# Hyena filter spectra from folded taps, with the frequencies ordered by parity

## The reference

```python
def _hyena_filter(L, p):                 # L = 256, HY_WIDTH = 512
    ...
    filt = (hdn @ p['hy_w3']).reshape(L, 2, HY_WIDTH)
    decay = jnp.exp(-t * jnp.abs(deltas))
    return filt * decay[:, None, :]

def _long_conv(u, filt, bias):
    taps = jnp.concatenate([filt[:, 0], jnp.zeros((1, HY_WIDTH)), filt[:0:-1, 1]], axis=0)
    kf = jnp.fft.rfft(taps, n=2 * L, axis=0)
    uf = jnp.fft.rfft(u, n=2 * L, axis=1)
    y = jnp.fft.irfft(uf * kf[None], n=2 * L, axis=1)[:, :L]
    return y + u * bias
```

## Time and profile before

| what | us |
|---|---|
| median of 3 runs | 1240.18 |
| lowest and highest run | 1238.13, 1241.17 |
| span of the profiled execution, first to last instruction | 1237.0 |
| PE busy in it | 1199.5 |
| DVE busy | 821.1 |
| ACT busy | 523.2 |

### The profile page before, as it was taken

How to read it: one execution, slowest core, us unless ns; L and a number is a source line. 1 busy time by engine, 2 the same in 40 slices (tenths; PEclk the granted TensorE clock), 3 DMA queues, 4 the chain that set the end, 5 groups by cost and what they waited for, 6 DMA issues and landing times. The chain is left out here.

```text
span 1237.0 us, 16729 instructions
## 1 busy us (share of the span) xinstructions
PE 1199.5 (97%) x6774; PEld 961.6 (78%) x6774; DVE 821.1 (66%) x1287; ACT 523.2 (42%) x907; POOL 1.7 (0%) x8
## 2 busy tenths in 40 slices
PE   6999999999999999999999999999999998999998
PEld 4666877777677788888887788778888788889887
DVE  5654357969766737767656656566589876776674
ACT  4452535452544432322122223347566455443454
POOL 0000000000000000000000000000000000000000
PEclk9999999999999999999999999999999999999999
DMA  9832333421011155555565454323343223665653
GB/s 337 274 120 85 131 125 113 161 85 51 18 35 52 53 172 182 188 204 181 181 213 187 154 185 164 94 68 102 103 119 120 69 62 111 201 186 183 186 179 120
DMA packets 132388, 171.82 MB, mean 139 GB/s; under 512 B 9268, under 2 KB 112342, under 8 KB 132312
## 3 DMA queue, kind: packets, MB, share of 16 engines
q1 hardware_dynamic: 131828, 170.58, 42.6%
q10 hardware_dynamic: 484, 0.18, 0.1%
HBM read 169.69 MB, written 1.05 MB: 138 GB/s over the span
## 5 line engine op out<-in xcount | busy, mean ns | idle before, releaser
L1812 DVE TENSOR_TENSOR w_lo<-w_raw,w_hi 128x1024 fp32r<-128x1024 f32 (+1 forms) x220 | 263.7, 1203 | 173.6 <-ACT w_hi L1439 171.5
L1439 ACT ACTIVATE w_hi<-w_raw 128x1024 fp32r<-128x1024 f32 (+1 forms) x220 | 228.4, 1042 | 337.5 <-DMA w_raw<-in_w_gu_dram 141.9
L700 PE MATMUL ps<-h_hi,w_hi 128*128 128x512 f32 (+1 forms) x576 | 218.7, 380 | 1.5 <-DVE xbc L1984 1.0
L702 PE MATMUL ps<-h_hi,w_lo 128*128 128x512 f32 (+1 forms) x576 | 212.6, 369 | 0.0
L701 PE MATMUL ps<-h_lo,w_hi 128*128 128x512 f32 (+1 forms) x576 | 212.4, 369 | 0.0
L700 PE MATMUL ps<-f_hi,w_hi 128*128 128x512 f32 (+1 forms) x472 | 167.7, 355 | 2.1 <-DVE xT L2216 1.6
L702 PE MATMUL ps<-f_hi,w_lo 128*128 128x512 f32 (+1 forms) x472 | 162.5, 344 | 0.0
L700 PEld LDWEIGHTS ps<-h_hi,w_hi 128*128 128x128 f32 x576 | 108.5, 188 | 27.7 <-issue 9.4
L702 PEld LDWEIGHTS ps<-h_hi,w_lo 128*128 128x128 f32 x576 | 108.4, 188 | 18.7
L701 PEld LDWEIGHTS ps<-h_lo,w_hi 128*128 128x128 f32 x576 | 108.6, 189 | 17.4
L711 PE MATMUL ps<-h_hi,w_hi 128*128 128x512 f32 x320 | 113.2, 399 | 0.4 <-ACT gate L1744 0.4
(11 more groups left out here) (342 smaller groups left out, 1905.0 us busy)
## 6 DMA issues: line engine op xcount, KB each, us to landing
w_raw<-in_w_gu_dram SPq DMA_DIRECT2D x88, 512.0 KB, 3.5
w_raw<-in_w_in_dram SPq DMA_DIRECT2D x60, 512.0 KB, 3.7
w_raw<-in_w_down_dram SPq DMA_DIRECT2D x32, 512.0 KB, 3.5
m_even<-in_w_mod_dram SPq DMA_DIRECT2D x14, 1024.0 KB, 5.7
m_odd<-in_w_mod_dram SPq DMA_DIRECT2D x14, 1024.0 KB, 5.7
m_raw<-in_w_mod_dram SPq DMA_DIRECT2D x24, 512.0 KB, 5.5
m_first<-in_w_mod_dram SPq DMA_DIRECT2D x16, 512.0 KB, 10.1
w_raw<-in_w_out_dram SPq DMA_DIRECT2D x16, 512.0 KB, 3.4
```

The costliest lines, as they stand in the source:

```text
L700: mm(o, w_hi[:, i % RING, w], hi[:, 0:n], start=first and k == 0, stop=False)
L702: last = mm(o, w_lo[:, i % RING, w], hi[:, 0:n], start=False, stop=final and k == nk - 1)
L1439: A(w_hi[:, i % RING, w], w_raw[:, i % RING, w], ACT.Copy).then_inc(w_hi_done, 1)
L1812: TT(w_lo[:, i % RING, w], w_raw[:, i % RING, w], w_hi[:, i % RING, w].bitcast(F32), ALU.subtract).then_inc(w_lo_done, 1)
```

## The change

The taps are folded once more before they meet the table. A tap of lag t and its mirror image at lag 256 - t have the same cosine at even frequencies and the opposite one at odd frequencies (and the other way round for sines). So the second block of lags is laid out as the mirror image of the first, and the sum and the difference of the blocks are formed on DVE: four new rows `plus`, `minus`, `odd_sum`, `even_diff` in `t_folds`, and a changed `t_diff`. Lag 0 and lag 128, which have no partner, are handled by columns of signs. The frequencies are ordered by parity (multiples of 4, then the other even ones, then the odd ones), in the inverse tables too. Then each spectrum needs 128 folded lags in place of 256: three spectra are one product each, and two (c = 0 and c = 4) are two products with 64 output rows each, from `plus` and `minus`.

`c_fwd` shrinks from 2 x 768 to 643 columns; three of these are the sign columns. `taps_ready` is signalled behind the fold in both layers. The core of the diff:

```diff
-    fwd = np.concatenate([cos, alt, sin[:, 1:], 0 * alt, sin[:, 1:P], alt, cos[:, 1:P]], axis=1)
-    fwd = fwd.reshape(2, P, 6 * P).transpose(1, 0, 2)
+    even, odd = np.concatenate([np.arange(0, L, 4), np.arange(2, L, 4)]), np.arange(1, L, 2)
+    order = np.concatenate([even, odd])
+    angle = 2 * np.pi * np.arange(P)[:, None] * order / (2 * L)
...
+    fwd = np.concatenate([cos, sin, nyquist, 1.0 - 2.0 * first, first - 1.0, 1.0 - first], axis=1)
...
+    lags = np.concatenate([np.arange(P + 1), np.arange(L - 1, P, -1)])
...
-        c_fwd = at("c_fwd", 187, [2, 6 * P])
+        c_fwd = at("c_fwd", 187, [5 * P + 3])
...
+        t_folds = [at(f"t_fold{l}", kb, [4, 512]) for l, kb in enumerate((104, 156))]
...
+                def spectrum_of_taps(c, bank):
+                    plus, minus, odd_sum, even_diff = (t_folds[l][:, j, :] for j in range(4))
+                    if c in (0, 4):
+                        for half, src in enumerate((plus, minus)):
+                            last = mm(ps[64 * half:64 * half + 64, bank, :], c_fwd[:, c * P + 64 * half:c * P + 64 * half + 64], src,
+                                      start=True, stop=True)
+                    else:
+                        src = (odd_sum, even_diff, (t_diff, t_diff1)[l][:, 0, :])[c - 1]
+                        last = mm(ps[:, bank, :], c_fwd[:, c * P:(c + 1) * P], src, start=True, stop=True)
+                    p.sig(last, "spectra_psum")
...
-                    col, src = ((0, t_sum), (P, t_sum), (4 * P, t_diff), (3 * P, t_diff), (5 * P, t_sum))[c]
-                    for t in range(2):
-                        last = mm(ps[:, ACC, :], c_fwd[:, t, col:col + P], src[:, t, :], start=(t == 0), stop=(t == 1))
-                    p.sig(last, "spectra_psum")
+                    spectrum_of_taps(c, ACC)
...
-                    for b, col, src in ((0, 0, t_sum1), (1, P, t_sum1), (2, 4 * P, t_diff1), (3, 3 * P, t_diff1), (7, 5 * P, t_sum1)):
-                        for t in range(2):
-                            last = mm(ps[:, b, :], c_fwd[:, t, col:col + P], src[:, t, :], start=(t == 0), stop=(t == 1))
-                        p.sig(last, "spectra_psum")
+                    for c, bank in enumerate((0, 1, 2, 3, 7)):
+                        spectrum_of_taps(c, bank)
...
+            def fold_taps(l, sums, diffs):
+                plus, minus, odd_sum, even_diff = (t_folds[l][:, j, :] for j in range(4))
+                sign, other, rest = (c_fwd[:, 5 * P + j:5 * P + j + 1] for j in range(3))
+                p.link(TT(even_diff, diffs[:, 0, :], diffs[:, 1, :], ALU.subtract))
+                p.link(TT(plus, sums[:, 0, :], sums[:, 1, :], ALU.add))
+                p.link(STT(out=minus, in0=sums[:, 1, :], scalar=sign, in1=sums[:, 0, :], op0=ALU.mult, op1=ALU.add))
+                p.link(STT(out=odd_sum, in0=sums[:, 1, :], scalar=other, in1=sums[:, 0, :], op0=ALU.mult, op1=ALU.add))
+                p.settle()
+                p.sig(STT(out=diffs[:, 0, :], in0=diffs[:, 0, :], scalar=rest, in1=diffs[:, 1, :], op0=ALU.mult, op1=ALU.add), "taps_ready")
...
-                        p.sig(TT(t_sum[0:1, 0, :], t_sum[0:1, 0, :], t_hyb[0:1, :], ALU.add), "taps_ready")
+                        p.chain(TT(t_sum[0:1, 0, :], t_sum[0:1, 0, :], t_hyb[0:1, :], ALU.add))
+                        dve.wait_ge(consts_full, 64)
+                        fold_taps(0, t_sum, t_diff)
                         p.own("taps_ready")
...
-                        p.sig(TT(t_sum1[0:1, 0, :], t_sum1[0:1, 0, :], t_hyb1[0:1, :], ALU.add), "taps_ready")
+                        p.chain(TT(t_sum1[0:1, 0, :], t_sum1[0:1, 0, :], t_hyb1[0:1, :], ALU.add))
+                    else:
+                        fold_taps(1, t_sum1, t_diff1)
```

More of the change, by code:

```diff
@@ L210, in constants @@
     k = np.arange(L)[None, :].astype(np.float64)
-    cos, sin = np.cos(2 * np.pi * k * t / (2 * L)), np.sin(2 * np.pi * k * t / (2 * L))
     alt = (-1.0) ** t
-    fwd = np.concatenate([cos, alt, sin[:, 1:], 0 * alt, sin[:, 1:P], alt, cos[:, 1:P]], axis=1)
-    fwd = fwd.reshape(2, P, 6 * P).transpose(1, 0, 2)
+    even, odd = np.concatenate([np.arange(0, L, 4), np.arange(2, L, 4)]), np.arange(1, L, 2)
+    order = np.concatenate([even, odd])
+    angle = 2 * np.pi * np.arange(P)[:, None] * order / (2 * L)
+    cos, sin = np.cos(angle), np.sin(angle)
+    sin[0, P:] = np.sin(np.pi * odd / 2)
+    nyquist = np.concatenate([alt[:P], cos[:, 1:P]], axis=1)
+    first = (i == 0)[:, None]
+    fwd = np.concatenate([cos, sin, nyquist, 1.0 - 2.0 * first, first - 1.0, 1.0 - first], axis=1)
     w = np.where(k == 0, 1.0, 2.0)
     mid = 2 * np.pi * k * (t[:P] - (L - 1) / 2) / (2 * L)
-    fold = np.concatenate([np.cos(mid), alt[:P], np.sin(mid)[:, 1:]], axis=1).reshape(P, NFREQ, P)
-    unfold = np.concatenate([(np.cos(mid) * w).T, alt[:P].T, 2 * np.sin(mid)[:, 1:].T], axis=0) / (2 * L)
+    fold = [np.cos(mid), np.concatenate([alt[:P], np.sin(mid)[:, 1:]], axis=1)]
+    unfold = [(np.cos(mid) * w).T / (2 * L), np.concatenate([alt[:P].T, 2 * np.sin(mid)[:, 1:].T], axis=0) / (2 * L)]
+    fold = np.concatenate([v[:, order] for v in fold], axis=1).reshape(P, NFREQ, P)
+    unfold = np.concatenate([v[order] for v in unfold], axis=0)
     inv = np.concatenate([fold, unfold.reshape(NFREQ, P, P).transpose(1, 0, 2)], axis=1)
+    lags = np.concatenate([np.arange(P + 1), np.arange(L - 1, P, -1)])
     tl = np.linspace(0.0, 1.0, L, dtype=f4)[:, None]
@@ L223, in constants @@
     arg = (fl * wl).astype(f4).astype(np.float64)
-    feats = np.concatenate([tl, np.cos(arg), -np.sin(arg)], axis=-1).T
+    feats = np.concatenate([tl, np.cos(arg), -np.sin(arg)], axis=-1)[lags].T
     deltas = np.linspace(np.log(1e-2) / 1.5, np.log(1e-2) / 0.3, 512, dtype=f4)
-    decay = np.exp((-tl * np.abs(deltas)).astype(f4).astype(np.float64)).reshape(2, P, 512).transpose(1, 0, 2)
+    decay = np.exp((-tl * np.abs(deltas)).astype(f4).astype(np.float64))[lags].reshape(2, P, 512).transpose(1, 0, 2)
     freq = (10000.0 ** (-np.arange(0, 32, 2) / 32)).astype(f4)
@@ L2400, in half_taps @@
                 def half_taps(t):
-                    if t == 1:
-                        p.own("taps_ready")
-                    else:
+                    if t == 0:
                         dve.wait_ge(wdt_split, 2)
```

## The result

Medians: 1240.11 us before (22 runs, 1238.13 to 1243.84) and 1243.50 us after (22 runs, 1239.99 to 1247.84). The ratio is 1.0023, with an interval of 1.0016 to 1.003: some 2 to 4 us slower, which is less than the 0.3% that the prediction took as the least difference a measurement can tell, and above its 1241.5 us. Beside the last experiments the changed kernel came out at 1.0032 (1.0018 to 1.0046). So five products a layer are gone, 8 us of work by the prediction's count, and the kernel is not faster at all.

The account below looks back on a forecast made before the run. TensorE, busy 97% of the span, was taken as the bound. Terms -0.4 - 0.7 + 0 + 2 x 1.2 = +1.3 on a 1237.0 us span gave 1238.3, plus 3.2 to the median: 1241.5 us, range 1237.0 to 1245.0.

Parts of the forecast that it names:

- The clock: Behind PE's gaps in layer 0 and at layer 1's start: clock falls, +1.2 us each, ends 0 and 2.3.
- The smaller table: Near the program's start: c_fwd shrinks from 768 to 322 KB, so weights queued behind it come sooner, -0.4 us.
- Layer 0 without the clock: Layer 0's spectra: fold on PE's path +3.3 us, fewer products -4.0 us, together -0.7 us.
- The products of layer 1: Layer 1's start: products end earlier, but PE waits for the same copy until 808.5; gain 0, new gap 4.2 us.
- The fold in the feed-forward part: Layer 1's fold behind L2414: of 3.3 us, 1.0 fits in front and 2.3 push DVE, covered; cost 0.
- rival by which layer 1 pays: Layer 1's start: copies come as soon as their products, L804 starts 4 us earlier without gap; 1235 us, chance 0.04.
- case without falls: Both PE gaps, layer 0 and layer 1's start: neither lets the clock fall; 1239.1 us, chance 0.10.
- slower rival: Both gaps: low clock wholly on work, 2.3 us each, table gives nothing, fold takes 3.7; 1244.5 us, chance 0.10.

Follow-up runs that it names:

- fold added: Kernel before with the five fold instructions added, unread, ahead of `taps_ready` in layer 0, products and table unchanged: 1245.50 us, ratio 1.0047.
- table padded: Changed kernel with the table c_fwd padded with zeros to its old 768 KB: 1242.19 us, 1.0032 times the kernel before.
- own banks: Changed kernel with layer 1's spectra on PSUM banks the first input products don't need at once: 1237.38 us, 0.9985 times the kernel before.
- layer 1 filled: Changed kernel with four idle products in the gap at the start of layer 1 alone: 1241.54 us, 1.0019 times the kernel before.
- both gaps filled: Changed kernel with four idle 128x512 products ahead of each of PE's two new waits: 1239.65 us, 1.0006 times the kernel before.
- the kernel before with both moves: Kernel before with layer 0's tap sums made earlier and layer 1's spectra on PSUM banks not needed at once: 1238.79 us, ratio 0.9991.
- third wait filled: Changed kernel, fold partly earlier, separate spectrum banks, two idle products before layer 1's second pair of squares in output projection: 1228.91 us, 0.9918 times before.

## Why the prediction was right where it was, and wrong where it was not

The sign and the mechanisms were right: two waits of about 4 us, nothing gained in layer 1, the clock falling behind both. The time came out some 2 us above the forecast, and three terms of the sum make that up: 0.8 to 1.6 us, 0.4 and 0.3. All three erred the same way, and the median stayed only 0.4 us under the 1243.9 from which the prediction would have called it slower.

- **The clock: right in kind, too small in size.** The step that took a fall at 1.2 us put some 2 us of a 4.6 us low stretch into the gap. In the profiled run of the changed kernel none of it lay there: the work came back at 1.00 and the 3.4 us behind it were all at half speed, 1.6 us lost in each layer. Where the clock did fall inside the gap (fold added, table padded, own banks, layer 1 filled), the low stretch was nearly 7 us instead, and 2.2 to 2.5 us were lost. So the outcome that was priced, part of a short stretch lying in the gap, occurred at these two places in no profiled run by more than 0.1 us; the bound named with 2.3 us was as near as the value taken. The 4.6 us from which both were worked out are the beginning of one execution, read from the pace of its transposes (the granted-clock column has 1.00 for that stretch). In the changed kernel's run both groups of sixteen there go at half pace (3.65 us from 10.17, 3.67 from 14.79), so the low level lasted to 18 us and more, as it did in nine of the fourteen profiled runs. Two falls are 3.2 to 4 us in place of 2.4. The granted clock says the same over all runs of a series: 0.994 beside 0.997 in the last comparison is (0.9972 - 0.9941) x 1240 = 3.8 us, all of the 3.3 by which the changed kernel was slower there.
- **The smaller table: 0 for -0.4.** The wait of 0.82 us that it should have shortened is 0.17 us in the changed kernel with either size of table. The step that failed is the reading of rows 8: a wait near the program's start, where the clock's rise and the first transfers differ between executions, was taken from one execution as a lasting price. The same goes for the half microsecond by which the weights came earlier in the changed kernel's run: in its second profiled run they came later than in rows 8.
- **Layer 0 without the clock: -0.40 for -0.7.** The fold is 3.44 us on the path where 3.3 was forecast: the add and subtract step at 0.61 as rows 7 said, but the three with a scalar at 0.66, not 0.64, the last taking 0.75. The products bring 3.65 to 3.8, not 4.0. The two halves do run side by side, but a pair with its changes of form costs 1.01 us, not 0.86 + 0.1.
- **The products of layer 1: 0, as forecast.** The copies stood where `hf` and `h_hi` put them and PE waited 3.74 us where 4.2 was said. The rival by which layer 1 pays is what the kernel with own banks does, by an edit that the change doesn't have.
- **The fold in the feed-forward part: 0, as forecast.** DVE at that place, then SP's modulation load and the next weight load, in the changed kernel:

```profile
722.26 1.21 DVE L2431 TENSOR_TENSOR hidden<-gate,ps 128x1024 f32<-128x1024 f32 x1
...
728.51 2.52 DVE L1832 TENSOR_TENSOR w_lo<-w_raw,w_hi 128x1024 fp32r<-128x1024 f32 x2
```
```profile
728.55 0.37 SPq L496 DMA_DIRECT2D m_even<-in_w_mod_dram  x1
730.72 0.37 SPq L463 DMA_DIRECT2D w_raw<-in_w_down_dram  x1
```

  Against rows 7 all of this is moved by the 1.35 us by which PE is later here anyway. The modulation load comes 3.67 later, so 2.3 by the push, just the forecast; the weight load behind it 1.35, so it was covered, and DVE is back in step with the second of the two splits that begin at 728.51 (over at 731.03; rows 7 and the 1.35 give 731.35).
- **Of the rivals**, the case without falls, 1239.1, is the kernel with both gaps filled (1239.65, ratio 1.0006). The slower rival (1244.5) was priced at 2.3 us a fall, the size measured where the clock fell early; the changed kernel's median lies between it and the forecast.

The Trainium skill's page "TensorE: Matmul & The Clock Gate", section "Why this matters for your kernels", was the rule that spoke against the change: idle gaps between bursts put the clock back. The traces agree, with 0.51 behind both gaps and 1.00 once these were filled; at the third wait the clock fell in six executions of thirteen.

What stays open: why the clock falls in one execution inside the gap and in another behind it, and at the wait of 2.4 us in some executions only. No kernel here was made to tell that. The differences elsewhere in the profiled runs (the kernel before with both moves lost 2.6 us behind 854.6, of which a fall at the third wait is some 1.7) were not followed either.

## What to carry to other kernels

Work that is taken from an engine which is then kept waiting buys nothing by itself: look first at what lets that engine go on, and move it (here a fold made in idle time and a choice of PSUM banks, 0.9918 of the time before with the third wait filled, and still 0.9932 without). On a kernel that keeps TensorE at full clock, price each new wait of a few microseconds not as the wait alone but with the work behind it at half speed, 1.6 to 2.5 us here. Where such a wait can't be removed, idle products in it are a cheap test of that price; here the clock stayed at its full level behind every gap that was filled, though the time followed clearly only where both gaps were.

## What the runs showed of the hardware that was not expected

- A wait of 2.3 to 2.7 us, at the same place in thirteen profiled executions, ended at full clock in seven of them and with 3.4 us of low clock in six. One execution is no proof that a wait of some length is harmless; the prediction had used it as one.
- The low stretches behind a wait lasted either about 3.4 or nearly 7 us (107.6 to 111.0 after, 104.8 to 111.6 in the kernel before with the fold), the longer ones all where the fall came before the work; of the short ones two also began before it, by 0.1 and 0.3 us.
- An fp32 product of 64 output rows in one column half and its partner in the other cost 1.01 us as a pair, with the changes of form, where a full product of 128 rows costs 0.86.
